# Down, output and o products with stationary weights on a residual that keeps channels on partitions

## The reference

```
for l in range(2):
    x = x + 0.5 * swiglu(rms_norm(x), w_gate, w_up, w_down)       # "ffn1"
    z = rms_norm(x) @ w_in                                         # "in": q, k, v, two convolutions
    x = x + concat([diff_attention, conformer_conv, short_conv]) @ w_out   # "out"
    hq = rms_norm(x) @ xa_wq;  kv = rms_norm(mem) @ xa_wkv          # "q", "kv"
    x = x + cross_attention(hq, kv) @ xa_wo                        # "o"
    x = x + 0.5 * swiglu(rms_norm(x), ...)                         # "ffn2"
return rms_norm(x) * final_norm
rms_norm(x) = x * rsqrt(mean(x*x over channels) + 1e-6) * g
```

## Time and profile before

| | us |
|---|---|
| median of 3 runs | 1141.22 |
| lowest and highest | 1140.66, 1141.96 |
| the profiled execution | 1141.1 |
| its span, first to last instruction | 1139.3 |
| TensorE busy | 1131.4, 6180 matmuls |
| weight loads busy | 976.9 |
| VectorE, ScalarE busy | 857.4, 647.1 |
| mean granted TensorE clock | 0.999 |

### The profile page before, as it was taken

One profiled execution on the slowest core, in us unless ns is written; L12 is line 12 of the kernel. 1 busy time (PEld: TensorE's weight loads), 2 busy tenths in 40 slices (PEclk: granted clock), 3 DMA queues, 4 the chain that ended last, 5 costly groups with the idle time before them and its releaser, 6 DMA issues.

```text
span 1139.3 us, 15680 instructions
## 1 busy us (share of the span) xinstructions
PE 1131.4 (99%) x6180; PEld 976.9 (86%) x6180; DVE 857.4 (75%) x1164; ACT 647.1 (57%) x937; POOL 21.8 (2%) x63
## 2 busy tenths in 40 slices
PE   9999999999999999999999999999999999999997
PEld 8888888888889888888888888888888898888886
DVE  7877676899967686766777676669998676866765
ACT  6555556547755554544565555464577556645454
POOL 1000000000000000000000000000000000000000
PEclk9999999999999999999999999999999999999999
DMA  7966654644444366555547655544545444666561
GB/s 265 327 202 188 218 186 147 221 149 165 170 159 172 111 224 217 164 201 199 186 151 255 219 161 205 192 165 168 186 148 204 166 146 125 210 190 216 183 200 43
DMA packets 66266, 210.92 MB, mean 185 GB/s; under 512 B 5009, under 2 KB 24209, under 8 KB 61073
## 3 DMA queue, kind: packets, MB, share of 16 engines
q1 hardware_dynamic: 65216, 209.26, 54.0%
q10 hardware_dynamic: 976, 0.66, 0.2%
HBM read 208.85 MB, written 1.05 MB: 184 GB/s over the span
## 4 chain that ended last, share of the span: by engine, by line
PE 94%; DVE 4%; DVEq 1%; ACT 0%; issue 0%
PE G L1720 28%; PE G L1729 14%; PE D L1567 10%; PE D L1565 10%; PE D L1566 10%; PE G L1660 3%; PE G L1565 3%; PE G L1567 3%; PE G L1566 3%; PE D L1660 2%; DVE w_lo L1006 2%; PE G L1669 1%; DVE acc L1215 1%; PE D L1669 1%; PE D L1632 1%; DVEq L1217 1%
## 5 line engine op out<-in xcount | busy, mean ns | idle before, releaser
L1006 DVE TENSOR_TENSOR w_lo<-w_raw,w_hi 128x2048 fp32r<-128x2048 f32 (+3 forms) x260 | 452.6, 1746 | 54.8 <-ACT w_hi L595 54.0
L595 ACT ACTIVATE w_hi<-w_raw 128x2048 fp32r<-128x2048 f32 (+3 forms) x260 | 381.1, 1475 | 35.2 <-PE D L1567 17.0
L1720 PE MATMUL G<-a,w_hi 128*128 128x512 f32 x1406 | 346.3, 391 | 0.1
L1720 PEld LDWEIGHTS G<-a,w_hi 128*128 128x128 f32 x1406 | 256.1, 188 | 48.6 <-issue 1.1
L1729 PEld LDWEIGHTS G<-a,w_lo 128*128 128x128 f32 x1406 | 175.4, 188 | 8.6
L1729 PE MATMUL G<-a,w_lo 128*128 128x256 f32 x1406 | 177.5, 277 | 0.0
L1111 DVE TENSOR_TENSOR zqk<-G,zqk 128x512 f32<-128x512 f32 x88 | 60.8, 691 | 127.3 <-ACT zqk L674 123.3
L1565 PE MATMUL D<-w_hi,hT_hi 128*128 128x512 f32 x352 | 137.2, 390 | 0.0
L1567 PE MATMUL D<-w_hi,hT_lo 128*128 128x512 f32 x352 | 137.0, 389 | 0.0
L1566 PE MATMUL D<-w_lo,hT_hi 128*128 128x512 f32 x352 | 136.9, 389 | 0.0
L674 ACT ACTIVATE zqk<-G 128x512 f32<-128x512 f32 x88 | 52.2, 593 | 143.1 <-PE G L1729 143.1
(11 more groups left out here) (261 smaller groups left out, 1282.5 us busy)
## 6 DMA issues: line engine op xcount, KB each, us to landing
w_raw<-w_dram SPq DMA_DIRECT2D x120, 1024.0 KB, 5.0
w_raw<-w_dram SPq DMA_DIRECT2D x143, 512.0 KB, 5.3
m_raw<-memT_dram SPq DMA_DIRECT2D x2, 1024.0 KB, 8.8
w_raw<-w_dram SPq DMA_DIRECT2D x6, 256.0 KB, 6.5
w_raw<-w_dram SPq DMA_DIRECT2D x8, 128.0 KB, 3.8
vx<-mem_dram SPq DMA_DIRECT2D x1, 1024.0 KB, 10.8
x<-x_dram SPq DMA_DIRECT2D x2, 256.0 KB, 5.7
gbc<-fin_dram SPq DMA_DIRECT2D x1, 512.0 KB, 6.6
```

The source lines that it names most:

```text
L595: A(w_hi[:, part(i)], w_raw[:, part(i)], ACT.Copy).then_inc(s_hi, 1)
L1006: V.tensor_tensor(w_lo[:, part_lo(i)], w_raw[:, part(i)], w_hi[:, part(i)].bitcast(F32), ALU.subtract).then_inc(s_lo, 1)
L1720: last = M(banks[b], whi[:, at:at + P], both, start=k == 0 and not low_first, stop=k == KD - 1 and low_first, skip_group_check=low_first)
```

## The change

x is kept with channels on partitions, `x[P, KD, T]`. Down (three of four FFNs), out and o products have stationary weights: for each of 8 channel tiles d the weights `w_hi`, `w_hi` again and `w_lo` are loaded, and the activations' hi, lo and hi stream past in 256 columns each (`channel_products`). `last_down` goes tile by tile and signals each bank; VectorE updates x bank by bank, ScalarE and VectorE make `a` from x. The transposes between stages go. The squares of x are summed over the eight channel tiles on VectorE (`channel_squares`), and over partitions by two fp32 products with a column of ones (`mean_squares` on TensorE), just before the last pair of k in the next stage; ScalarE copies the result to SBUF for GpSimd. `rinv_diag` moves behind the split of chunk 2's weights, the broadcast into the middle of chunk 2. In the last FFN down keeps its old form on its own hidden tiles, x enters its PSUM banks by 16 fp32 products with twice the identity (`residual_by_token`), and the final norm reads PSUM. The first x is loaded by token into a tile shared with the memory, transposed as before, and copied from PSUM by ScalarE. Activations of out and o lie in `b`, 192 B behind `a` in the same room; other tiles are moved by small pads, `LINE` is 64.

```diff
+OFF = 48
+TURN = 16
...
-LINE = 128
+LINE = 64
...
-        x = sb("x", [P, TT, D])
-        a = sb("a", [P, KD, 2, T], F32R)
-        a_hi, a_lo = a[:, :, 0, :], a[:, :, 1, :]
+        x = sb("x", [P, KD, T])
+        a_room = sb("a", [P, 2 * KD * T + OFF], F32R)
+
+        def activations(at):
+
+            both = a_room[:, at:at + 2 * KD * T].rearrange("p (k a t) -> p k a t", k=KD, a=2)
+            return both, both[:, :, 0, :], both[:, :, 1, :]
+
+        a, a_hi, a_lo = activations(0)
+        b, b_hi, b_lo = activations(OFF)
+        hT_room = sb("hT", [P, 2 * SLOTS_H * T + TURN], F32R)
+
+        def hidden_places(at):
+
+            both = hT_room[:, at:at + 2 * SLOTS_H * T].rearrange("p (a s t) -> p a s t", a=2, s=SLOTS_H)
+            return both[:, 0], both[:, 1]
+
+        hT_hi, hT_lo = hidden_places(0)
+        rows_hT = hidden_places(TURN)
...
+        def channels(d):
+
+            return DB[d // 2][:, d % 2 * T:(d % 2 + 1) * T]
...
+                def high(j):
+
+                    act.wait_ge(s_xup, 4 * (q - 1) + j + 1)
+                    for k in (2 * j, 2 * j + 1):
+                        A(to[:, k, :], x[:, k, :], ACT.Copy, scale=gain(NORMS[q % 4], k)).then_inc(s_ahi, 1)
+
+                def squares(j):
+
+                    A(squared[j // 2][:, j % 2, :], x[:, 2 * j:2 * j + 2, :].rearrange("p k t -> p (k t)"), ACT.Square,
+                      scale=D ** -0.5).then_inc(s_sq, 1)
+
+                high(0)
+                high(1)
+                squares(0)
+                high(2)
+                squares(1)
+                high(3)
+                squares(2)
+                squares(3)
...
+            def mean_squares(q):
+
+                act.wait_ge(s_stat, q)
+                A(mean_sq[:, :], STAT_BANKS[q % 4][:, 0:TT], ACT.Copy).then_inc(s_ssq, 1)
...
-                act.wait_ge(s_end, p + 1)
-                A(junk[:, lo:hi], x[:, t, lo:hi], ACT.Square, scale=D ** -0.5, accum_out=ssf[:, p:p + 1]
+                act.wait_ge(s_piece, p + 1)
+                A(junk[:, lo:hi], DB[2 * (lo // N) + t][:, :], ACT.Square, scale=D ** -0.5, accum_out=ssf[:, p:p + 1]
...
+            def x_update(q, j):
+
+                if j < 3:
+                    dve.wait_ge(s_bank, 3 * q + j + 1)
+                else:
+                    dve.wait_ge(s_blk, last_of(q // 4, LAST_STAGES[q % 4]) + 1)
+                xs = x[:, 2 * j:2 * j + 2, :]
+                V.scalar_tensor_tensor(xs, pair(DB[j]), FACTORS[q % 4], xs, ALU.mult, ALU.add).then_inc(s_xup, 1)
...
+                x_update(q - 1, 1)
+                for k in range(0, 2):
+                    low_part(q, k)
+                x_update(q - 1, 2)
+                for k in range(2, 4):
+                    low_part(q, k)
+                x_update(q - 1, 3)
+                for k in range(4, 8):
+                    low_part(q, k)
+
+            def channel_squares(q):
+
+                dve.wait_ge(s_sq, 4 * q)
+                V.tensor_tensor(v_sb[:, :, :], v_sb[:, :, :], gbc[:, :, :], ALU.add)
+                dve.drain()
+                V.tensor_tensor(v_sb[:, 1, :], v_sb[:, 0, :], v_sb[:, 1, :], ALU.add)
+                dve.drain()
+                V.tensor_tensor(channel_sum, v_sb[:, 1, 0:T], v_sb[:, 1, T:], ALU.add).then_inc(s_chsum, 1)
...
+                    channel_squares(4 * l + 3 * f)
+                    split(l, stage, ("gu", 2, 0, 8))
+                    if 4 * l + 3 * f == 4 * L - 1:
+                        twice_identity()
                     rinv_diag(l, f)
-                    split(l, stage, ("gu", 2, 0, 8))
                     pair_sum(l, f, 0)
...
+            def channel_products(d, hi, lo, whi, wlo, n, k, start, stop):
+
+                w = slice(n * D + d * P, n * D + (d + 1) * P)
+                M(channels(d), whi[:, w], hi[:, k, :], start=start and d % 2 == 0, stop=False, skip_group_check=True)
+                M(channels(d), whi[:, w], lo[:, k, :], start=False, stop=False, skip_group_check=True)
+                return M(channels(d), wlo[:, w], hi[:, k, :], start=False, stop=stop, skip_group_check=True)
...
             def last_down(q, hi, lo, ks):
 
                 whi, wlo = weights(last_of(q // 4, LAST_STAGES[q % 4]))
+                for d in range(KD):
+                    for n, k in enumerate(ks):
+                        last = channel_products(d, hi, lo, whi, wlo, n, k, False, n == 1)
+                    if d in (1, 3, 5):
+                        last.then_inc(s_bank, 1)
+                last.then_inc(s_blk, 1)
...
-                            if (c, n, t) == (1, 1, 1):
-                                pe.wait_ge(s_xup, 4 * q + 2)
-                                x_transposes(q + 1, range(4))
...
+            def residual_by_token():
+
+                pe.wait_ge(s_twice, 1)
+                pe.wait_ge(s_ssq, 4 * L)
+                for k in range(KD):
+                    for t in range(TT):
+                        M(DB[2 * (k // 4) + t][:, k % 4 * P:(k % 4 + 1) * P], x[:, k, tok(t)], twice,
+                          start=k % 4 == 0, stop=False, skip_group_check=True)
...
+                pe.wait_ge(s_chsum, q)
+                for t in range(TT):
+                    last = M(STAT_BANKS[q % 4][:, t:t + 1], channel_sum[:, tok(t)], ones[:, 0:1], start=t == 0, stop=True,
+                             skip_group_check=True)
+                last.then_inc(s_stat, 1)
...
                     for k in range(0, KD, 2):
-                        if k == 2:
-                            second_transposes(q)
+                        if k == 6:
+                            mean_squares(q)
                         gate_up(l, f, 0, range(k, k + 2), ready=8 * q)
...
+                def down_pair(c):
+
+                    down_chunk(c)
+                    down_chunk(c + 1)
 
                 for c in range(2, STEPS):
                     pe.wait_ge(s_sum, chunk(l, f, c - 2))
-                    for ks in late_parts(l, f, c):
-                        gate_up(l, f, c, range(*ks), low_first=ks[0] == 2 if (q, c) == (0, 2) else c % 2 == 1)
-                        if (q, c, ks) == (0, 2, (0, 2)):
-                            rinv_broadcast()
+                    if c % 2 == 0:
+                        for ks in late_parts(l, f, c):
+                            gate_up(l, f, c, range(*ks), low_first=ks[0] == 2 if (q, c) == (0, 2) else False,
+                                    middle=rinv_broadcast if q and c == 2 else None)
+                            if (q, c, ks) == (0, 2, (0, 2)):
+                                rinv_broadcast()
+                    else:
+                        for ks in late_parts(l, f, c):
+                            gate_up(l, f, c, range(*ks), low_first=True)
+                    if c == 3 and rows:
+                        residual_by_token()
                     if c % 2 and c < STEPS - 2:
-                        down_chunk(c - 3)
-                        down_chunk(c - 2)
-                down_chunk(STEPS - 4)
-                down_chunk(STEPS - 3)
-                hidden_ready(LAST)
+                        down_pair(c - 3)
```

More of the change, by code:

```diff
@@ L254, in hymba_kernel @@
         e_sb = sb("e_sb", [P, 2, 2, T])
+        squared = (v_sb, gbc)
+        channel_sum = v_sb[:, 1, 0:T]
+        twice = std[:, 0:P]
         junk = e_sb[:, :, :, :].rearrange("p c a t -> p (c a t)")
@@ L513, in _ @@
                     sp.dma_start(const[:, K_DIST:], const_d[:, K_DIST:]).then_inc(s_const, 16)
+                if (l, stage, n) == (0, "ffn1", ("down", 4)):
+                    sp.wait_ge(s_xT, KD)
+                    sp.wait_ge(s_ssq, 1)
+                    sp.wait_ge(s_first, 2)
                 if (stage, n) == ("ffn1", ("down", 4)):
@@ L1601, in down @@
                         between()
-                    for c in range(2):
-                        w = slice(n * D + c * N, n * D + (c + 1) * N)
-                        for t in range(TT):
-                            last = product(DB[2 * c + t][:, :], hi[:, k, tok(t)], lo[:, k, tok(t)], whi[:, w],
-                                           wlo[:, w], start and n == 0, False)
+                    for d in range(KD):
+                        last = channel_products(d, hi, lo, whi, wlo, n, k, start and n == 0, False)
                 last.then_inc(s_blk, 1)
@@ new lines, in token_products, with token_down @@
+            def token_products(c, t, hi, lo, whi, wlo, n, k, stop):
+                w = slice(n * D + c * N, n * D + (c + 1) * N)
+                M(DB[2 * c + t][:, :], hi[:, k, tok(t)], whi[:, w], start=False, stop=False, skip_group_check=True)
+                M(DB[2 * c + t][:, :], hi[:, k, tok(t)], wlo[:, w], start=False, stop=False, skip_group_check=True)
+                return M(DB[2 * c + t][:, :], lo[:, k, tok(t)], whi[:, w], start=False, stop=stop, skip_group_check=True)
+            def token_down(l, stage, i, hi, lo, k):
+                whi, wlo = weights(INDEX[l, stage, i])
+                for c in range(2):
```

(6 more changed lines are left out.)

304 lines of the change are left out of this document (144 added, 160 removed).

## The result

The changed kernel takes 1145.65 us (median of 5 runs, 1145.28 to 1146.72); the kernel before, on the same chip, 1140.69 (1140.51 to 1141.96). The ratio is 1.0042, with a 95% interval of 1.0028 to 1.0056: slower by 5.0 us. Forecast were 1146.7 us.

What follows compares the result with a forecast made beforehand. TensorE, busy for 99% of the span, was taken as the bound. 8.7 + 0.8 - 11.1 - 0.6 + 2.8 + 2.55 + 3.2 - 0.75 = +5.6 us gave 1146.7 us, own range 1143.5 to 1150, over all cases 1134.5 to 1151.

Steps and rivals of the forecast that it cites:

- Down, output and o blocks: 1176 products of 512 columns become 2352 of 256, at 117 ns each: +8.7 us, bounds 0 and 15.3.
- the 512-column stretch ahead: Down pairs stand behind 16 products of 512 columns, first ground for taking 117 ns instead of 113.3.
- Rival A: Down runs at the quick 113.3 ns pace, by other addresses or a long run: 1138.0 us; chance 0.35.
- The double load: Down loads one stationary tile twice, then its partner, like the cross-attention scores at 0.1167 us; second ground for 117 ns.
- Rival B: Down runs at the 120 ns pace, stationary load and moving read in each other's way: 1153.3 us; chance 0.05.
- The fixed share of 2.5 ns for each matmul: On TensorE, the skill's per-matmul share would make 1176 more matmuls cost 2.9 us; the quick run does not show it.
- Return to 512 columns: First 512-column products behind a 256-column run are slower by 0.03 us, some 31 times more often: +0.8 us.
- Transposes: Seven stage boundaries lose 16 transposes each, 0.79 us for eight: -11.1 us.
- Mean squares: Seven times two one-column fp32 products on TensorE, 28 instructions at 0.10 us: +2.8 us, bounds 0.8 and 3.4.
- The chain in the FFN heads: Chunk 2's first product waits for VectorE's sum behind the diagonals, 0.85 us three times: +2.55 us, bounds 0 and 4.
- Residual by token: In the last FFN, 16 fp32 products, 32 instructions at 0.10 us: +3.2 us, once.
- Tail: At the kernel's end the last update goes and the square starts on PSUM: about 0.75 us earlier.

Runs made afterwards that it cites:

- experiment 1: Changed kernel with odd chunks ahead of down pairs in the first three FFNs ordered 14 short, 14 long, 2 short, 2 long products: 1139.64 us.
- experiments 2 and 3: Changed kernel with 4 short, 4 long products ahead of the down pairs: 1140.32 us; with 8 short, 8 long: 1147.06 us.
- experiment 7: Changed kernel with the one-column mean-square products and the 16 residual products of the last FFN each made twice: 1152.04 us.
- Experiment 6: Changed kernel with VectorE's sum of chunk 0 put ahead of the inverse root's diagonals in the FFN heads: 1144.53 us.
- experiment 10: Changed kernel with 2-short-2-long leads ahead of down pairs and cross scores, sum ahead of diagonals, two memory-value products held into out: 1138.98 us.

## Why the prediction was right

*Down, output and o blocks.* Forecast +8.7 at 117 ns, measured +6.8 and +1.9. That the sum fits to a tenth is in part luck, as two errors cancel. Down ran at 117.8, which is 1.3 us more than 117 gives for its 1584 products. Output went at 117.8 too, but for 0.20 us at the first product behind each group of transposes. And o ran at 113.3 for long stretches of the first layer, which I had not foreseen and which made up for it. The last 96 products of o, first in layer one, then in layer two:

```profile
378.29 0.28 PE L1665 MATMUL D<-a,w_hi 128*128 128x256 f32 x1
...
389.18 0.42 PE L1817 MATMUL G<-a,w_hi 128*128 128x512 f32 x1
```

```profile
942.92 0.28 PE L1665 MATMUL D<-a,w_hi 128*128 128x256 f32 x1
...
954.23 0.39 PE L1817 MATMUL G<-a,w_hi 128*128 128x512 f32 x1
```

10.89 us and 11.31: 113.4 and 117.8 ns each, for the same order of instructions in both layers. In the first layer the pace changed at 361.6 us, in the middle of a run of short products without a long one, five products behind one that had held TensorE for 0.16 us. What turned it no run isolates.

For down the reason given, the 512-column stretch ahead, was the right one: experiment 1 moves that alone and the pace follows, experiments 2 and 3 bound it. The prediction leaned on "every 256-column run behind eight or more 512-column products went at the slower pace to its end". That was read too widely: behind 20 long ones the kernel before runs 12 scores at 117 ns and then, in the same run, 16 short query products (346.34 to 348.16) at 113.7. Rival A (1138.0) named the pace that experiment 1 then reached, at 1139.64; its conditions, other addresses or a long run, were not what decides in down. The double load, which I had counted as second ground for 117 ns, decides nothing: with it unchanged, both paces occur. Rival B's pace appeared when the distance was made a multiple of 256 B; I had looked for multiples of 512.

The fixed share of 2.5 ns for each matmul (the Trainium skill, TensorE: Matmul & The Clock Gate, "Wait — 56ns, not 53.3ns?") is not in these traces: at the quick pace a halved product takes 113.6 ns, half of 226.7 being 113.4.

*Return to 512 columns.* Some 0.02 us each (0.55 us for 30 more in experiment 1), against 0.03. The changed kernel has 26 more of them than the one before, not 31, so about 0.5 us against 0.8.

*Transposes.* Forecast -11.1, measured -10.9, and +11.6 when doubled.

*Mean squares.* 2.5 us in their own row against 2.8. The first 512-column product behind each of the seven groups loses 0.08 more, 0.6 us in all, which is what the prediction had set off against the stalls behind the transposes. The load-like price of one column held (0.11 us for each instruction added in experiment 7, against 0.10).

*The chain in the FFN heads.* The place and the order of events were right. Counted from the head's start (389.18), the mean squares start at 8.4 us (forecast 8.2) and the sum is there at 12.0 (12.1). The step that missed is TensorE's arrival: ready for chunk 2 at 11.6, not 11.3, as the small products and the returns to 512 columns hold it up too. So the wait is 0.46 us, and the next product takes 0.06 more than it took before (0.34 against 0.28): 1.6 for three instead of 2.55. Experiment 6 took back 1.1.

*Residual by token.* 3.5 against 3.2, at 0.11 instead of 0.10 each.

*Tail.* -0.9 against -0.75. The last store is issued 2.49 us behind the last matmul's start (1139.22, 1141.71); forecast 2.75.

*Not foreseen.* The self-attention scores of the first layer wait 0.37 us longer for VectorE, as those of the second layer did before. And the profiled execution has the late load in it. The median, 1145.65, is 1.05 us under the forecast. Of these, 0.4 is the base: the forecast started from 1141.1, and the median of the kernel before is 1140.69. The change itself cost 5.0 us against 5.6. The heads alone are 1.0 us under the forecast; the smaller errors (+0.2 transposes, -0.3 mean squares, +0.3 residual, -0.3 returns, +0.4 scores, -0.15 tail) cancel nearly, and the rest lies within what the runs can tell.

## What to carry to other kernels

Halving the columns of a product is free only at the quick pace: before doing it, look in the timeline for the distance between starts behind each kind of predecessor. Try two or four long products between short ones ahead of the long run of short ones, and look at every place afterwards: ahead of down it worked each time, elsewhere not always, and a pace won in one place can be lost in the next. A mean over a few dozen products hides which pace they had, as one long gap behind transposes can make up the difference: read single starts. Keep the moving tile off multiples of 256 B from the weights (64 B off was enough here). A tiny fp32 product costs TensorE as much as one of 128 columns, and where a chain through three engines ends on an engine that also owes TensorE a sum, put the sum ahead of it.

## What the runs showed of the hardware

- 256-column fp32r products with a new weight load each ran at one of three steady paces in down, gate and up, and input blocks, at a granted clock of 0.999 throughout: 113.5, 117.8 and 119.6 to 119.9 ns. 512-column products run at 226.7.
- In the down pairs the 512-column products ahead set which of the first two it is (2 and 4: 113.5; 8 and 16: 117.8), and it held over 48 and 96 products. Elsewhere that is not enough: o had the same order in both layers and ran at 113.3 in the first, at 117.8 in the second. The pace can survive four fp32 transposes (113.5 behind the first group in experiment 10) or be gone behind them (117.8 behind the second). What carries it, no run shows.
- The third pace came in down with a distance of a multiple of 256 B between moving tile and weights, behind 16 long products and behind 2 (119.9 and 119.6 ns). Why, no run shows.
- An fp32 product of one column is two instructions. Added ones cost 0.11 us each, as with 128 columns.
- The first 256-column product behind four fp32 transposes holds TensorE for 0.20 us, the first 512-column one behind a group of fp32 instructions for 0.31 instead of 0.23.
